# Four weight-split subtractions moved from VectorE to GpSimd in a transformer block kernel

## What is computed

```python
h = modulate(rmsnorm(x, norm1_g), sh1, sc1)
q, k, v, hy_in, cf_in = split(h @ w_in)
attn = neighbourhood_attention(q, k, v, k_ctx, v_ctx, rpb)   # 8 heads, 256 + 256 keys
hy = hyena_mixer(hy_in, ...)                                 # two long convolutions through an FFT
cf = conformer_conv(cf_in, ...)                              # 31 taps, layer norm, silu
x = x + g1 * concat(attn, hy, cf) @ w_out
h2 = modulate(rmsnorm(x, norm2_g), sh2, sc2)
x = x + g2 * expert_choice_ffn(h2, router_w, w1, w3, w2)     # 16 experts, 32 tokens each
return rmsnorm(x, final_norm_g)
```

## Time and profile before

| | |
|---|---|
| time, median of 3 runs | 1409.22 us (1406.94 to 1411.07) |
| profiled execution: time / span | 1409.22 us / 1407.4 us |
| PE busy | 1045.3 us (74%) |
| PE weight loads | 567.3 us (40%) |
| DVE busy | 473.5 us (34%) |
| ACT busy | 285.5 us (20%) |
| POOL busy | 56.4 us (4%) |
| moved by DMA | 487.32 MB, mean 346 GB/s |
| mean granted PE clock | 0.886 |

### The profile page before, as it was taken

One profiled execution on the slowest core, in us unless ns is written; L12 is line 12 of the kernel. 1 busy time (PEld: TensorE's weight loads), 2 busy tenths in 40 slices (PEclk: granted clock), 3 DMA queues, 4 the chain that ended last, 5 costly groups with the idle time before them and its releaser, 6 DMA issues.

```text
span 1407.4 us, 16140 instructions
## 1 busy us (share of the span) xinstructions
PE 1045.3 (74%) x6960; PEld 567.3 (40%) x6960; DVE 473.5 (34%) x886; ACT 285.5 (20%) x495; POOL 56.4 (4%) x79
## 2 busy tenths in 40 slices
PE   9999999999999997565666656666566665565566
PEld 7887786799877852111111111111112111111113
DVE  5867777787878321010110101101011010110103
ACT  6536665644345210000000000000000000000001
POOL 0005300000000000000000000000000000000000
PEclk9999999999999999788887878878887787988869
DMA  9655169343533889999999999999999999999995
GB/s 376 230 217 222 43 228 372 157 154 132 199 149 108 372 363 429 431 428 429 429 429 429 428 430 429 428 430 429 428 429 430 429 428 430 428 429 430 427 430 234
DMA packets 37343, 487.32 MB, mean 346 GB/s; under 512 B 4279, under 2 KB 5976, under 8 KB 7320
## 3 DMA queue, kind: packets, MB, share of 16 engines
q1 hardware_dynamic: 36152, 484.71, 82.5%
q10 hardware_dynamic: 1120, 1.57, 0.3%
HBM read 485.22 MB, written 1.05 MB: 346 GB/s over the span
## 4 chain that ended last, share of the span: by engine, by line
DMA 49%; PE 35%; DVE 10%; ACT 3%; issue 2%; POOL 1%; DVEq 0%; SPq 0%; ACTq 0%
PE ps L272 34%; DMA ring<-in_expert_w 28%; DMA late<-in_expert_w 10%; DMA few<-in_expert_w 10%; DVE xT L1709 2%; DMA ring<-in_pieces 2%; DVE ring_r L326 1%; ACT ring_r L320 1%; DVE V L1677 1%; DVE ring L588 1%; POOL hT L772 0%; PE ps L1719 0%; DVE sm L1377 0%; DVE V L1673 0%; DVE U L1677 0%
## 5 line engine op out<-in xcount | busy, mean ns | idle before, releaser
L272 PE MATMUL ps<-ring,G 128*32 128x512 f32 x608 | 106.1, 834 | 76.7 <-DMA ring<-in_expert_w 76.7
L272 PE MATMUL ps<-late_r,ring_r 128*128 128x256 f32 x832 | 154.6, 285 | 2.8 <-DVE hT_r L497 1.7
L272 PE MATMUL ps<-ring,hT 128*32 128x512 f32 x608 | 100.8, 797 | 72.6 <-DMA ring<-in_expert_w 72.6
L272 PEld LDWEIGHTS ps<-late_r,ring_r 128*128 128x128 f32 x832 | 129.8, 190 | 7.5 <-issue 4.6
L272 PE MATMUL ps<-hT_r,ring_r 128*128 128x256 f32 x400 | 113.1, 283 | 0.0
L326 DVE TENSOR_TENSOR ring_r<-ring,ring_r 128x2048 fp32r<-128x2048 f32 (+1 forms) x44 | 98.6, 2275 | 29.5 <-ACT ring_r L320 29.3
L272 PE MATMUL ps<-U_r,ring_r 128*128 128x256 f32 x480 | 107.0, 283 | 0.4 <-DVE hT_r L505 0.3
L272 PE MATMUL ps<-late,U 128*128 128x256 f32 (+2 forms) x402 | 86.7, 490 | 20.5 <-DMA late<-in_expert_w 9.3
L272 PE MATMUL ps<-late,G 128*32 128x512 f32 (+1 forms) x352 | 61.2, 771 | 38.7 <-DMA late<-in_expert_w 38.7
L272 PEld LDWEIGHTS ps<-ring,G 128*32 128x32 f32 x608 | 19.6, 131 | 162.2 <-DMA ring<-in_expert_w 126.3
L320 ACT ACTIVATE ring_r<-ring 128x2048 fp32r<-128x2048 f32 (+1 forms) x44 | 81.7, 1897 | 9.7 <-DMA ring<-in_pieces 7.2
(11 more groups left out here) (327 smaller groups left out, 1244.9 us busy)
## 6 DMA issues: line engine op xcount, KB each, us to landing
ring<-in_expert_w SPq DMA_DIRECT2D x115, 2048.0 KB, 45.9
late<-in_expert_w SPq DMA_DIRECT2D x57, 2048.0 KB, 45.7
ring<-in_pieces SPq DMA_DIRECT2D x20, 2048.0 KB, 8.8
few<-in_expert_w SPq DMA_DIRECT2D x19, 2048.0 KB, 45.9
ring<-in_wmodt SPq DMA_DIRECT2D x8, 2048.0 KB, 8.3
ring<-in_wmodk SPq DMA_DIRECT2D x4, 2048.0 KB, 8.8
ring<-in_pieces SPq DMA_DIRECT2D x2, 1024.0 KB, 7.7
ring<-in_pieces SPq DMA_DIRECT2D x1, 1792.0 KB, 12.0
```

The source lines that it names most:

```text
L272: mm = lambda e, o, l, r, st, sp_=True, sk=False: e.matmul(o, l, r, start=st, stop=sp_, skip_group_check=sk)
```

## The change

DVE's list loses the four `conv` calls in steps 3, 4, 5 and 7 of the attention stage. POOL's list gets the same four chunks: 41, 42 and 43 between its first and its second Hyena multiply, and chunk 44 behind the second. `conv_lo` itself is the same function, called with another engine: it waits for `w_hi`, subtracts, and raises `w_lo`. Since `w_lo` is now raised by two engines, POOL first waits until DVE has brought it to 40.

```diff
--- before.py
+++ after.py
@@ -2440,8 +2440,6 @@
                 dve_na_norm(e, i - 1)
             if i == 6:
                 dve_hy_mul(e, 1)
-            if i in (3, 4, 5, 7):
-                conv({3: 42, 4: 43, 5: 44, 7: 45}[i])
             if i == 3:
                 dve_cf_norm(e)
             if i == 4:
@@ -2499,7 +2497,11 @@
         e.memset(CF[:, :, 0:15], 0.0).then_inc(s["pad"], 1)
         e.memset(CF[:, :, 271:286], 0.0).then_inc(s["pad"], 1)
         pool_hy_mul(e, 0)
+        e.wait_ge(s["w_lo"], 40)
+        for k in (41, 42, 43):
+            conv_lo(e, k)
         pool_hy_mul(e, 1)
+        conv_lo(e, 44)
         for ex in range(16):
             pool_expert(e, ex)
```

## The result

The change costs 10.5 us: 1419.23 us (median of 5 runs, 1417.05 to 1420.56) against 1408.71 us (5 runs, 1406.94 to 1411.07), ratio 1.0072 with a 95% interval of 1.0055 to 1.0088. The profiled execution took 1419.62 us, span 1417.8, mean clock 0.885.

A forecast was written before the change was run, and what follows sets the result against it. DVE and PE were nearly joint bounds in the attention part, weight loads bound the experts; 8.2 us of waiting plus 1.0 us of clock made +9.2 on 1409.22 us, so 1418.4 us, range 1410 to 1423.

The forecast's parts named there:

- POOL's price: One 2048-column subtraction on POOL was to take 4.5 us, with 5.08 us as the upper end.
- Holding for the whole length: A 4.5 us POOL instruction keeps DVE's operations with two SBUF inputs and fast scalings waiting until it ends.
- Rival (a): POOL's long operations don't hold DVE long, or DVE mostly gets in first: 1406.8 to 1409.5 us; chance 0.17.
- Chunk 41 free: DVE's scaling of 414.17 waits until 418.1, before the Hyena gate begins at 419.7: cost 0, 0.3 us to spare.
- Chunk 42: DVE's product of 420.20 comes 0.04 us too late and starts at 424.5; the row maximum behind it is 3.7 late.
- Chunk 43: DVE's two-input product at 431.0 waits until 435.1; the next maximum is 5.6 late, scores 6 on PE 4.9 late.
- Chunk 44: DVE's product of 442.56 asks at 446.41, waits until 450.75; PE's transposes of 445.15 move to 453.3, 8.2 us late.
- The clock: Behind PE's gap of about 4.5 us before 453.3, the lower clock costs 1.0 us, between 0 and 1.7.
- Rival (c): Some of the three DVE collisions are missed: 1415.1 us, or 1411.3 to 1413.7 if only the last bites; chance 0.22.
- Rival (d): Three collisions, with two more clock falls or a POOL price of 5.1 us: +15 us; chance 0.57 together with the forecast.
- Relief: From 410 to 452 us the chain of waits credits DVE with 4.40 us, but PE's gaps allow only 2.45 us.
- rival (b): The chain of waits is right and PE's busy time isn't a floor, so subtraction time comes back: 1404.8 us; chance 0.04.

The follow-up runs named there:

- run 2: The change with each POOL subtraction cut into eight instructions of 256 columns: 1408.70 us against 1408.39 for the kernel before, ratio 1.0002.
- run 1: Kernel before, all subtractions still on DVE, plus four POOL additions of a zero column to 2048 columns: 1418.93 us against 1408.39, ratio 1.0080.
- Run 6: Kernel before with chunk 41 alone moved to POOL, behind its first Hyena multiply: 1408.41 us against 1408.68, ratio 0.9995.
- Run 3: The change plus 17 unread PE matmuls in the gap before step 8's transposes: 1416.85 us against 1408.39 for the kernel before, ratio 1.0064.
- run 4: The change with chunk 44 back on DVE in step 7: 1412.31 us against 1408.39 for the kernel before, ratio 1.0026.
- run 7: Kernel before, all four subtractions on DVE, but chunks 42 to 44 later: 1407.70 us against 1408.68, ratio 0.9992.
- run 8: Kernel before with chunks 42 to 44 later on DVE and ACT's conformer square ahead of its rounding in step 2: 1406.39 us against 1408.85, ratio 0.9985.

## Why the prediction was right, point by point

- **POOL's price.** 4.5 us by the rows of 384 and 512 columns; 4.51 to 4.57 measured. Output in fp32r shows no extra cost: the f32 rows had given 4.51, and one piece of 256 columns in run 2 takes 5.90 / 8 = 0.74 us, where POOL's f32 additions of 256 columns take 0.73 (L774, at 116.09 before).
- **Holding for the whole length.** It was my reading, from blocked pieces of at most 1.38 us. It holds at 4.5 us (the DVE rows above), costs as much where no work left DVE (run 1), and goes when the instruction is cut (run 2). Rival (a) is out.
- **Chunk 41 free.** Run 6: 0.0 us.
- **Chunk 42.** The gate at 420.20 was forecast to lose by 0.04 us, and it did (419.36 against POOL's 419.31). So close a call could have been luck, but the product loses in runs 3 and 4 too (4.75 us in both). The maximum behind it is 3.70 us late; forecast 3.7.
- **Chunk 43.** Here one step was wrong in its place. POOL was forecast at 430.8 (it is 430.75 with the offset), the reciprocal ahead of the products at 428.5 (428.44). But then I let the scaling L1319 pass and had the second L1317 caught. The rows show L1319 itself held for 4.74 us. I had sorted it as harmless, as it has one SBUF input, and its time before looked no faster than the 0.42 us of a product; its row of before:

```profile
429.20 0.41 DVE L1319 TENSOR_SCALAR late<-late,PC 128x256 f32<-128x256 f32 x1
```

  The next maximum is 5.80 us late (forecast 5.6), scores 6 are 5.27 late (4.9), their maximum 4.13 (3.85): the walk was off by 0.2 to 0.4 us in these steps, and by 0.2 at the end of it. That the wrong operation hardly moved the sum is luck: the scaling and the second product stand next to each other, and either would have waited until POOL's end.
- **Chunk 44.** L1334 held, asked at 446.69 in the time of before (forecast 446.41). PE's transposes: 452.74 + 0.85 - 445.15 = 8.44 us late, forecast 8.2.
- **The clock.** This is the term that was mis-sized: 1.0 us, from 0 to 1.7. Behind the transposes the work to the next value product took 4.63 us before (445.15 to 449.78) and 7.17 us now (452.74 to 459.91): 2.54 us. Run 3 gives 2.57 us by taking it away. The value product of before:

```profile
449.78 1.09 PE L272 MATMUL ps<-S,V 128*64 128x128 f32 x16
```

  The bound of 1.7 was one row's 3.4 us at the low level; here PE worked at it for over 5 us. A second fall in the change comes behind the gaps of 1.81 and 0.85 us at 425 to 426.5:

```profile
428.00:430.00 2.00, 2.00 (x6) 0.92 (x5) 1.93 (x3) 2.00 (x3) 0.10 (x1) 0.50 0.00 0
```

  It cost nothing that the rows show. The next maximum (435.26) followed DVE's own work without a wait for PE, the chain of waits runs from 418.85 to that maximum through DVE alone, and PE then waited 0.88 us for the exponential before scores 6.
- **Sum.** 8.2 + 1.0 = 9.2 forecast; 8.4 + 2.5 = 10.9 in the stretch and 10.5 between the medians. Rival (c) is out, as all three collisions came. Rival (d) isn't borne out: POOL took 4.5 us, and of two clock falls only one cost time. Its +15 would have been 1424 us, above the range's own end of 1423.
- **Experts.** One for one, as forecast: the expert phase moved 429 GB/s in both, and lasts 913.3 and 913.6 us.
- **Relief.** The limit of 2.45 us by PE's gaps was right and the chain's 4.40 us was not (runs 7 and 8). That is rival (b) out: with DVE relieved and no subtraction on POOL, 1.1 us of the stretch come back, 1.7 with ACT's order changed.

What stays open: which engine goes first when both ask within 0.1 us. L1319 is recorded as started at 429.83 and was held by a POOL instruction recorded at 429.90. Also not tried is chunk 42 or 43 alone, so their 4.3 us aren't divided.

## What to carry to other kernels

Before moving work from DVE to an idle POOL, lay the two timelines over each other: in this kernel each long POOL subtraction or addition in SBUF held the next DVE operation that has two SBUF inputs or is a scaling in SBUF, until it ended. What decides is the length of one instruction and whether somebody waits for the held one, not POOL's busy share; cut in pieces of 256 columns the same work was free within noise, at 1.4 times its POOL time. And where the chain of waits credits an engine with more than the other bound has in gaps, take the gaps as the limit.

## What was not expected of the hardware

- A scaling of 256 columns with two per-partition scalars (L1319, 0.41 us alone) is held by POOL: 4.74 us in the change, 0.80 us beside pieces. A reciprocal from SBUF to SBUF of the same size is not: 1.74 us in run 2, where POOL's pieces ran beside most of it, 1.75 without.
- POOL's 2048 columns cost 4.52 us with two full operands and 3.60 us when one operand is a repeated column (and the output f32, not fp32r; the two weren't varied apart). Eight pieces of 256 cost 5.90 us, and 6.26 to 6.42 us for the other three chunks.
- A gap of 4.05 us on PE was followed by over 5 us of work at 1.2 GHz, worth 2.5 us where PE is the bound. Gaps of 1.81 and 0.85 us brought the low level too.
